# Inverse of the delta rule: late taps divided between ScalarE with GpSimd and VectorE, GpSimd's head tiles behind level 0, level 5 updated in place, norm sums at other steps

## What is computed

```
z = rms_norm(x) @ w_in                      # q,k,v for attention; conv input; q,k,v,gate,a,b for the delta rule
y_conv = silu(layer_norm(causal_depthwise_conv(val * sigmoid(gate), dw[31 taps]) + bias))
g = cumsum(-exp(a_log) * softplus(a + dt_bias))        # per head and chunk
m = strict_lower((k*beta) @ k.T * decay)               # per head and chunk
u, w = solve(m + I, [v*beta, k*beta*exp(g)])           # unit lower triangular
intra = lower(q @ k.T * decay)
for each chunk: v_new = u - w @ state
                out = (q*exp(g)) @ state + intra @ v_new
                state = state*exp(g_last) + (k*exp(g_last-g)).T @ v_new
x = x + rms_norm(concat(y_attn, y_conv, gated norm of out) @ w_out)
```

## Time and profile before

| | us |
|---|---|
| median of 3 executions | 2652.47 (2650.78 to 2653.61) |
| profiled execution, its own time | 2650.35 |
| its span | 2648.6 |
| VectorE busy | 1530.4 |
| ScalarE busy | 1089.3 |
| GpSimd busy | 114.6 |

### The profile page before, as it was taken

The page is one execution under the profiler, slowest core; times in us unless marked ns, Lnnn a source line. Parts: engine busy times, 40 slices in busy tenths (PEclk is TensorE's granted clock), DMA queues, the critical chain, the costliest instruction groups (busy, mean ns, idle before and its releaser), DMA issues.

```text
span 2648.6 us, 36760 instructions
## 1 busy us (share of the span) xinstructions
PE 2560.8 (97%) x12966; PEld 2027.1 (77%) x12966; DVE 1530.4 (58%) x1981; ACT 1089.3 (41%) x1570; POOL 114.6 (4%) x103
## 2 busy tenths in 40 slices
PE   7999999999999999999998899999899989899998
PEld 5767888887668888886687778888676778688886
DVE  4656755756566736646975554344559865543444
ACT  4554433435554424432473443233423734432323
POOL 1000000000000000000210010000102100100000
PEclk9999999999999999999998999999999999999998
DMA  4203332333113333342220223333221201233333
GB/s 132 72 1 95 95 105 86 100 98 92 41 34 95 103 94 95 102 112 64 56 64 3 64 72 105 92 95 105 54 80 48 72 10 50 76 101 92 95 99 91
DMA packets 394592, 208.04 MB, mean 79 GB/s; under 512 B 9738, under 2 KB 392660, under 8 KB 394484
## 3 DMA queue, kind: packets, MB, share of 16 engines
q1 hardware_dynamic: 391396, 202.79, 26.5%
q0 software_dynamic: 2176, 3.06, 0.5%
q10 hardware_dynamic: 912, 0.77, 0.1%
HBM read 205.34 MB, written 2.10 MB: 78 GB/s over the span
## 4 chain that ended last, share of the span: by engine, by line
PE 88%; DVE 6%; ACT 3%; issue 1%; DMA 0%; POOL 0%; DVEq 0%; SPq 0%; ACTq 0%; POOLq 0%
PE ps L611 64%; PE ps L630 6%; PE ps L888 2%; ACT whi L1437 1%; DVE ps L2758 1%; DVE x_sb L2761 1%; PE ps L1041 1%; PE ps L1056 1%; DVE yc L2467 1%; PE ps L943 1%; PE ps L675 1%; PE ps L945 1%; PE ps L1216 1%; PE ps L944 1%; ACT lnt L1441 1%
## 5 line engine op out<-in xcount | busy, mean ns | idle before, releaser
L1437 ACT ACTIVATE whi<-raw 128x1024 fp32r<-128x1024 f32 (+1 forms) x354 | 395.8, 1119 | 1062.9 <-PE ps L611 947.6
L611 PE MATMUL ps<-h_hi,whi 128*128 128x512 f32 x1984 | 788.3, 397 | 4.7 <-ACT whi L1437 4.1
L611 PE MATMUL ps<-h_lo,whi 128*128 128x512 f32 x1984 | 772.7, 389 | 0.0
L611 PE MATMUL ps<-h_hi,wlo 128*128 128x512 f32 x1984 | 530.3, 389 | 0.0
L2065 DVE TENSOR_TENSOR wlo<-raw,whi 128x1024 fp32r<-128x1024 f32 (+1 forms) x354 | 458.5, 1296 | 55.5 <-ACT whi L1437 54.5
L611 PEld LDWEIGHTS ps<-h_hi,whi 128*128 128x128 f32 x1984 | 372.7, 188 | 89.6 <-ACT whi L1437 8.2
L611 PEld LDWEIGHTS ps<-h_lo,whi 128*128 128x128 f32 x1984 | 372.7, 188 | 82.5 <-issue 6.2
L611 PEld LDWEIGHTS ps<-h_hi,wlo 128*128 128x128 f32 x1984 | 372.4, 188 | 77.1
L611 PE MATMUL ps<-a_hi,whi 128*128 128x512 f32 x592 | 230.3, 389 | 0.0
L611 PE MATMUL ps<-a_lo,whi 128*128 128x512 f32 x592 | 230.3, 389 | 0.0
L2793 DVE TENSOR_TENSOR cv<-ps,rstd 128x512 f32<-128x512 f32 x88 | 60.9, 692 | 247.8 <-PE ps L611 241.0
(11 more groups left out here) (406 smaller groups left out, 3235.5 us busy)
## 6 DMA issues: line engine op xcount, KB each, us to landing
raw<-in_w_up SPq DMA_DIRECT2D x132, 512.0 KB, 3.8
raw<-in_w_down SPq DMA_DIRECT2D x64, 704.0 KB, 4.5
raw<-in_w_in SPq DMA_DIRECT2D x82, 512.0 KB, 3.8
raw<-in_w_gate SPq DMA_DIRECT2D x44, 512.0 KB, 3.8
raw<-in_w_o SPq DMA_DIRECT2D x16, 512.0 KB, 3.6
raw<-in_w_out SPq DMA_DIRECT2D x16, 512.0 KB, 3.7
xs<-in_x SPq DMA_DIRECT2D x2, 1024.0 KB, 6.7
out<-xs SPq DMA_DIRECT2D x3, 512.0 KB, 2.9
```

What stands on the lines that cost most here:

```text
L611: return pe.matmul(ps[:, ACC[s], :], w[s][:, k, :], r[:, k, :], start=start, stop=stop)
L1437: act.activation(whi[s][:, 0:kt, :], raw[s][:, 0:kt, :], ACT.Copy).then_inc(w_hi_ready.sem, 1)
```

## The change

- Late taps: VectorE keeps the eight of channel tile 0, all in the head slots (2, 3, 3). Those of tile 1 are made in steps 0 to 7 by two engines: ScalarE writes the scaled input into `kb[:, n % 2]`, GpSimd adds it to `yc[:, 1]`. ScalarE's copy n waits for GpSimd's addition n-2.
- GpSimd's `delta_head(h)` waits for `lt0_ready(h)` as well, the end of VectorE's L2512.
- VectorE's L2505 no longer waits for `turned_used`.
- Level 5 is updated in place in `xdT` like the levels before; `level_turned` and `level_second` read `xdT`. ScalarE copies the diagonal blocks into `xT` (two half tiles per head, in n = 18, 19, 22, 23), and L1277 waits for that.
- The norm's steps move: mean_sum 15 to 13, mean_kept 16 to 14, centring 18 to 16, squares 19 to 17, centered_sum 21 to 19, reciprocal root 22 to 21, scaling 24 to 23; merged_high 13, 14 to 8, 9; merged_low 16, 17 to 10, 11.

```diff
@@ gpsimd @@
                     pool.wait_ge(qk_ready.sem, qk_ready.at(L, h))
+                    pool.wait_ge(lt0_ready.sem, lt0_ready.at(L, h))
                     nc.gpsimd.tensor_tensor(gq[:, h, :], gq[:, h, :], eg[:, h % 2, :], ALU.mult).then_inc(gq_scaled.sem, 1)
...
+                for n in range(CT - TAPS_IN):
+                    pool.wait_ge(tap_scaled.sem, tap_scaled.at(L, n))
+                    if n >= 1:
+                        pool.wait_ge(late_tapped.sem, late_tapped.at(L, n - 1))
+                    nc.gpsimd.tensor_tensor(yc[:, 1, :], yc[:, 1, :], kb[:, n % 2, :], ALU.add)\
+                        .then_inc((late_tapped if n < CT - TAPS_IN - 1 else dw_ready).sem, 1)
@@ tensor @@
-                            mm = pe.matmul(ps[0:HB, ACC[n % 2], c], p1c[HB:P, n % 2, c], xT[HB:P, h, tb * P + HB:(tb + 1) * P],
+                            mm = pe.matmul(ps[0:HB, ACC[n % 2], c], p1c[HB:P, n % 2, c], xdT[HB:P, h, c],
...
-                            mm = pe.matmul(ps[0:HB, STAT[n % 2], c], xT[0:HB, h, tb * P:tb * P + HB], ident[0:HB, 0:HB], start=True, stop=True)
+                            mm = pe.matmul(ps[0:HB, STAT[n % 2], c], xdT[0:HB, h, c], ident[0:HB, 0:HB], start=True, stop=True)
...
                     pe.wait_ge(turned_used.sem, turned_used.at(L, GH - 1))
+                    pe.wait_ge(dw_ready.sem, dw_ready.at(L, NC - 1))
                     for i in range(NC):
-                        pe.wait_ge(dw_ready.sem, dw_ready.at(L, i))
...
-                    if n == 15:
+                    if n == 13:
                         mean_sum()
-                    if n == 21:
+                    if n == 19:
                         centered_sum()
...
                 for h in range(GH):
                     pe.wait_ge(x_new.sem, x_new.at(L, STEPS - GH + h))
+                    pe.wait_ge(diag_kept.sem, diag_kept.at(L, h))
@@ scalar @@
-                    if n in (13, 14):
-                        merged_high(n - 13)
-                    if n == 16:
+                    if n < CT - TAPS_IN:
+                        if n >= 2:
+                            act.wait_ge(late_tapped.sem, late_tapped.at(L, n - 2))
+                        else:
+                            act.wait_ge(kk_ready.sem, kk_ready.at(L, GH - 2 + n))
+                        k = TAPS_IN + n
+                        order.told(act.activation(kb[:, n % 2, :], ypad[:, 1, k:k + SEQ], ACT.Identity,
+                                                  scale=param(pd, L, D_DW + k * NC + 1)), tap_scaled, L, n)
+                    for h in {18: (0,), 19: (1,), 22: (2,), 23: (3,)}.get(n, ()):
+                        for r in range(2):
+                            rows_r = slice(HB * r, HB * (r + 1))
+                            ins = act.activation(xT[rows_r, h, :].rearrange("p (t d) -> p t d", d=P)[:, :, rows_r],
+                                                 xdT[rows_r, h, :].rearrange("p (t d) -> p t d", d=HB), ACT.Copy)
...
+                    if n in (8, 9):
+                        merged_high(n - 8)
+                    if n == 14:
                         act.wait_ge(mean_ready.sem, mean_ready.at(L, 0))
...
-                    if n == 19:
+                    if n == 17:
...
-                    if n == 22:
+                    if n == 21:
@@ vector @@
-                    dve.wait_ge(turned_used.sem, turned_used.at(L, h))
                     order.told(dve.tensor_tensor(gv[:, h, :], ps[:, STAT[0], :], dm[:, s, :], ALU.mult), intra_made, L, h)
...
-                    if n < STEPS - 2 * GH:
+                    if n < STEPS - GH:
                         order.told(dve.tensor_tensor(xdT[:, h, :], xdT[:, h, :], ps[:, ACC[n % 2], 0:TB * HB], ALU.subtract), x_new, L, n)
-                    elif n < STEPS - GH:
-                        for r in range(2):
-                            rows_r = slice(HB * r, HB * (r + 1))
-                            ins = dve.tensor_tensor(by_token(xT[rows_r, h, :])[:, :, rows_r], by_block(xdT[rows_r, h, :]),
-                                                    by_block(ps[rows_r, ACC[n % 2], 0:TB * HB]), ALU.subtract)
...
-                LATE = ((0, 2), (2, 6), (6, 10), (10, 10))
+                LATE = ((0, 2), (2, 5), (5, 8), (8, 8))
...
-                    if LATE[-1][1] <= n + 8 < 2 * (CT - TAPS_IN):
-                        late_tap(n + 8)
-                    if n == 18:
+                    if n == 16:
                         dve.wait_ge(mean_kept.sem, mean_kept.at(L, 0))
...
-                    if n == 24:
+                    if n == 23:
                         dve.wait_ge(ln_rs.sem, ln_rs.at(L, 0))
...
-                    if n in (16, 17):
-                        merged_low(n - 16)
+                    if n in (10, 11):
+                        merged_low(n - 10)
```

More of the change, by code:

```diff
@@ L108, in network @@
     LEVELS, HB = 7, P // 2
+    beside = [3, 3, 3, 2, 2, 2, 2, 2, 1, 1, 1, 1]
+    TAPS_IN = sum(beside)
     N_IN2 = 3 * NA + 2 * NC + 4 * GH
@@ L233, in network @@
         p1_ready, x_new, xpt_ready = (sem(n, STEPS) for n in ("p1_ready", "x_new", "xpt_ready"))
+        late_tapped, diag_kept = again(qkstat_ready, CT - TAPS_IN - 1), again(qkrs_ready, GH)
+        tap_scaled = again(vvsq_ready, CT - TAPS_IN)
         p1_masked, p1_turned, low_zeroed = sem("p1_masked", STEPS - GH), sem("p1_turned", GH), again(qksq_ready, 1)
@@ L1877, in _ @@
                         order.told(act.activation(xd[0:upto, (n - 2) % GH, :], ps[0:upto, STAT[n % 2], 0:TB * HB], ACT.Copy), xt_kept, L, n - 2)
-                    if n in (13, 14):
-                        merged_high(n - 13)
-                    if n == 16:
+                    if n < CT - TAPS_IN:
[11 more added lines that the diff above has]
+                                                 xdT[rows_r, h, :].rearrange("p (t d) -> p t d", d=HB), ACT.Copy)
+                            if r == 0:
+                                order.step(ins)
+                            else:
+                                order.told(ins, diag_kept, L, h)
+                    if n in (8, 9):
+                        merged_high(n - 8)
+                    if n == 14:
                         act.wait_ge(mean_ready.sem, mean_ready.at(L, 0))
                         order.told(act.activation(lnt[:], ps[:, TRN[0], :], ACT.Copy, scale=1.0 / CC), mean_kept, L, 0)
-                    if n == 19:
+                    if n == 17:
                         for i in range(NC):
@@ L2539, in level_updated @@
                     order.settle()
-                    if n < STEPS - 2 * GH:
+                    if n < STEPS - GH:
                         order.told(dve.tensor_tensor(xdT[:, h, :], xdT[:, h, :], ps[:, ACC[n % 2], 0:TB * HB], ALU.subtract), x_new, L, n)
-                    elif n < STEPS - GH:
-                        for r in range(2):
-                            rows_r = slice(HB * r, HB * (r + 1))
-                            ins = dve.tensor_tensor(by_token(xT[rows_r, h, :])[:, :, rows_r], by_block(xdT[rows_r, h, :]),
-                                                    by_block(ps[rows_r, ACC[n % 2], 0:TB * HB]), ALU.subtract)
-                            if r == 0:
-                                order.step(ins)
-                            else:
-                                order.told(ins, x_new, L, n)
                     else:
@@ L2557, in _ @@
                 unit_blocks = lev[:, LEVELS - 1, :].unsqueeze(1).to_broadcast([P, TB, HB])
-                beside = [3, 3, 3, 2, 2, 2, 2, 2, 1, 1, 1, 1]
-                TAPS_IN = sum(beside)
-                assert 2 * (CT - TAPS_IN) == 16
-                LATE = ((0, 2), (2, 6), (6, 10), (10, 10))
+                LATE = ((0, 2), (2, 5), (5, 8), (8, 8))
                 def late_tap(n):
-                    k, t = TAPS_IN + n // NC, n % NC
+                    k = TAPS_IN + n
                     order.settle()
-                    ins = dve.scalar_tensor_tensor(yc[:, t, :], ypad[:, t, k:k + SEQ], param(pd, L, D_DW + k * NC + t), yc[:, t, :],
+                    ins = dve.scalar_tensor_tensor(yc[:, 0, :], ypad[:, 0, k:k + SEQ], param(pd, L, D_DW + k * NC), yc[:, 0, :],
                                                    ALU.mult, ALU.add)
                     if k == CT - 1:
-                        order.told(ins, dw_ready, L, t)
+                        order.told(ins, dw_ready, L, 0)
                     else:
```

## The result

The changed kernel takes 2637.15 us (median of 5 executions, 2636.79 to 2639.72) where the kernel before takes 2652.47 (2650.18 to 2653.61): a ratio of 0.9946, 95% interval 0.9932 to 0.9961, a gain of 15.3 us. A second series gave 2638.54 against 2652.83, again 0.9946 (0.9932 to 0.9959). The forecast was 2637.1 us, a gain of 15.4. The profiled execution took 2636.79 us (its span is 2635.0), 13.6 less than the one before; for it 2635.0 had been forecast.

A forecast was written before the change was run, and what follows sets the result against it. TensorE's matmuls are busy 97% of the span, so time is won only where TensorE waits or runs at the lower clock. Layers' 9.35 and 6.05 make 15.4 us, 2652.47 becoming 2637.1; range 2633 to 2642, widened by rivals to 2630 to 2645.

The forecast's parts named there:

- A: Head 0's slot: VectorE's tiles and one tap fewer win time, less GpSimd's collision with the taps; 0.45 us per layer.
- the rival of the clock further back: Clock stays up from head 1's L1121 on, some 1.9 us per layer more; 2632 us, chance 0.09.
- B: Head 3 up to step 0: wait for ScalarE goes, two tiles get shorter, less a collision; 1.1 us per layer.
- C: Steps 0 to 4 of the inverse, with the clock at its upper level: 2.0 us in layer 0, 1.25 in layer 1.
- D: Steps 4 to 9: 8.60 us become five steps of 1.40, 7.0; 1.6 us won in each layer.
- The relay rival: GpSimd's additions held to 2.0 us make ScalarE wait, steps 2.05, 3.9 us per layer; 2645 us, chance 0.05.
- the low-clock rival: Clock falls as before and collisions cost in full; C, A, B and F lose 5.7 us; 2642.8 us, chance 0.14.
- E: Step 9 to the first L1277 takes 26.75 us: 3.5 us won in layer 0, 1.65 in layer 1.
- F: First products after the levels, clock still low at first: 0.7 us won in layer 0, 0 in layer 1.
- slower: Relay delays and TensorE's gaps of 0.65 per step keep the clock down; 2664.7 us, chance 0.04.
- nothing: The gain is given back in the products and norms behind the stage; chance 0.04.
- The rule weighed in the prediction: VectorE and GpSimd exclude each other for whole instructions: A's collision 1.7 instead of 1.3, A 0.05, time 2637.9 us.

The follow-up runs named there:

- experiment 2: The changed kernel with four taps instead of three in head 1's slot and two instead of three in head 2's; 2638.83 us.
- experiment 3: The changed kernel with all sixteen late taps on VectorE again, none of them on ScalarE and GpSimd; 2643.69 us.
- experiment 1: The changed kernel without GpSimd's wait for level 0's tiles; 2639.28 us.
- 4 to 11: Eight runs: the changed kernel with edits to the norm's steps, the diagonal copies or the level-5 update, or without any edit; 2628.75 to 2640.0 us.
- experiment 5: The changed kernel with ScalarE's diagonal copies of heads 1 to 3 moved behind the last `p1_turned`; 2635.40 us.
- experiment 8: The changed kernel with level 5 as in the kernel before: two half tiles on VectorE, no diagonal copies; 2635.57 us.
- experiment 6: The changed kernel with the norm's reciprocal root behind the last `p1_turned` and its scaling on VectorE behind the loop; 2628.75 us.
- experiment 9: The changed kernel again, unedited; 2638.54 us. Its event: TensorE's clock falls in the attention in some executions, 1.5 us.

## Why the prediction was right, and where it was not

- **A, term right, clock wrong.** The product in head 1's slot began 0.80 and 0.46 sooner, after 1.55 us of wait where 1.9 was forecast. The working holds: tiles 0.99, taps 3.66 for 3.11, together 0.44 up to `gz` (forecast 0.45); layer 0 adds a pause of 0.47 ahead of L2523 that is gone, 0.36 net. The remaining 1.6 per layer is the clock: the product takes 1.13, not 1.63 and 2.05, and the groups behind it run at the upper level too. The step that failed is that A counted nothing for the clock at this product: the gain stood only in the rival of the clock further back, with a chance of 0.09. It came in both layers, and its 1.9 per layer was near. The margin is seen in all traces: after waits of 2.02 (the kernel before, layer 1) and 2.37 to 2.73 us the clock fell, yet it held after 2.35 and 2.34 (experiments 2 and 3, layer 1). After 1.84 (experiment 1) it held in both layers, and after 1.55 to 1.57 in both layers of all nine traces with three taps and GpSimd's wait (the changed kernel and 4 to 11).
- **B, right.** The wait of 0.86 for ScalarE is gone, 0.71 for TensorE takes its place; `gv` comes 0.19 sooner and the tiles give 0.95. L2553 was held by 0.84, where 0.35 was charged net.
- **C and D, right.** Steps of 1.40, the clock at 1.00, additions of 1.27; TensorE's wait ahead of second(0) is 1.14, forecast 1.2. The relay rival is refuted: ScalarE waited for GpSimd nowhere in the levels. Of the low-clock rival only the tail came, which F had priced.
- **E, wrong: 28.45 / 28.28 instead of 26.75.** Up to first(20), at 1426.25, the layout is right (19.9, forecast 20.2). From there to L1289 are 8.57 instead of 6.5. The failed step is "xt_kept(19) ends at +2.65": it ended at +3.52, since head 1's copies, 0.85, stood ahead of it in ScalarE's queue, and I had given the early copies no time. The rest of ScalarE's list came as forecast, 0.9 late. The second miss is the product after p1_turned(3), 0.3 in my list: it ended 1.16 behind `p1_turned`, as it ran at the low clock behind its twin. L1289 came another 0.4 behind the last tile, not 0.1. Together 0.93 + 0.86 + 0.3 = 2.1, close to the gap of 2.07 (8.57 less 6.5). Experiments 5 and 8 take copies away or move them back (1.2 / 1.5 and 1.2 / 0.9 sooner at that product), experiment 6 the norm's pair and with it the low clock (2.1 / 1.9).
- **F, right in size.** The product takes 2.04. Experiment 6 shows that this was no property of the place: with the norm's pair behind the steps, and TensorE's 1.13 us of wait gone, it is 1.13.
- **The slower and the nothing rivals.** Neither came. The gain of the stages, 16.15, reached the end less 2.6, of which 1.5 is the event of experiment 9.
- **The total, in part luck.** A's 3.6 too little and E's 3.3 too much cancel. Then the profiled execution missed its own forecast by 1.8 (2636.79 for 2635.0); the median comes out within 0.1 because the kernel before's profile lay 2.1 below its median, which the forecast carried over, and the changed kernel's only 0.4.

The rule weighed in the prediction: taps of 3.66 beside 2.98 us of GpSimd, and L2553 at 1.26 instead of 0.42. The Trainium skill, "SBUF — State Buffer", section "Who interferes with whom", has such pairs excluding each other for a whole instruction. L2553's 0.84 agrees with that. The taps' 1.33 over 2.33 is the 1.3 that the prediction took from rows, but it does not speak against whole instructions: of the three taps the first took 1.18, the second 1.66, the third 0.75, and GpSimd's masking beside them 1.74 instead of 1.27:

```profile
1366.42 1.29 POOL L585 TENSOR_TENSOR gq<-gq,eg 128x512 f32<-128x512 f32 x1 [48.41 <-DVE gk L2541]
1367.66 1.74 POOL L588 TENSOR_TENSOR intraT<-intraT,tri 128x512 f32<-128x512 f32 x1
```

Each held tap ended some 0.55 us after the GpSimd instruction that held it, so its 0.75 began 0.2 ahead of that end. The prediction's 1.7 counted the two holds as 0.55 and 1.15, where they were 0.43 and 0.91.

## What to carry to other kernels

When work leaves an engine, lay out the queue of the engine that receives it, instruction by instruction, with nothing at zero: here 0.85 us of copies in ScalarE's tail undid an update made cheaper on VectorE. A wait of TensorE can be worth more than its length, since the clock may fall behind it (1.67 us more behind a tap of 0.8 in experiment 2), and less certainly so: price it at both clocks and give the better one its chance. An edit that only pays with another must be tried with it; GpSimd's wait brought nothing in one trace alone and 3.1 and 1.4 in company, the clock's part included.

## What the hardware showed that I had not expected

- The same wait does not give the same clock. After 2.40 us the eight matmuls in head 1's slot took 1.84, after 2.35 us 1.13, in one execution of one kernel; behind masked(0) it was 2.10 us in both layers of experiment 1, and the clock fell in one. In the attention of both layers the clock fell or held in code that no edit touched, for 1.5 us.
- Short waits can do it too: in the tail the granted clock was 0.77 with waits of 0.42 and 1.13 us between small groups, and 1.00 with 0.42 and 0.47.
- The five executions of the changed kernel lie 2.9 us apart in one series and 3.8 in the other. The two events in the attention are 1.5 each, and the program's start adds to it: TensorE's first matmul stands at 5.45 to 6.43 us in the fourteen traces, and in six of them the clock was also low from about 13 us on.
